# State-space stage of a hybrid transformer block: decay exponents from 16 contraction rows, both directions added before one mixing multiplication

## What is computed

```python
def ssd_chunked(x, dt, A, Bm, Cm):
    ...
    xdt = (x * dt[..., None]).reshape(b, c, CHUNK, G, r, P)
    adt = jnp.moveaxis((dt * A).reshape(b, c, CHUNK, G, r), 2, -1)
    a_cs = jnp.cumsum(adt, axis=-1)
    CB = jnp.einsum('bclgn,bcsgn->bcgls', Cc, Bc)
    Wd = CB[:, :, :, None] * segsum_exp(adt)
    y_diag = jnp.einsum('bcgrls,bcsgrp->bclgrp', Wd, xdt)
    ...
    return (y_diag + y_off).reshape(b, l, H, P)
...
    y_fwd = ssd_chunked(xs, dt[:, :, 0], A[0], Bm, Cm)
    y_bwd = fl(ssd_chunked(fl(xs), fl(dt[:, :, 1]), A[1], fl(Bm), fl(Cm)))
    y = y_fwd + y_bwd + d_skip.astype(f32)[:, None] * xs
```

## Time and profile before

| what | value |
|---|---|
| three runs | 2532.5, 2537.7, 2540.1 us (median 2537.7) |
| span of the profiled execution, first to last instruction | 2541.3 us |
| PE busy in it | 2338.2 us (92%) |
| DVE busy | 1483.2 us (58%) |
| ACT busy | 1006.7 us (40%) |
| POOL busy | 545.2 us (21%) |
| state-space stage | about 359 to 866 us of the span |

### The profile page before, as it was taken

How to read it: one execution, slowest core, us unless ns; L and a number is a source line. 1 busy time by engine, 2 the same in 40 slices (tenths; PEclk the granted TensorE clock), 3 DMA queues, 4 the chain that set the end, 5 groups by cost and what they waited for, 6 DMA issues and landing times.

```text
span 2541.3 us, 33250 instructions
## 1 busy us (share of the span) xinstructions
PE 2338.2 (92%) x12329; PEld 1957.3 (77%) x12329; DVE 1483.2 (58%) x2230; ACT 1006.7 (40%) x1608; POOL 545.2 (21%) x618
## 2 busy tenths in 40 slices
PE   7999989999999699989999999999988998969997
PEld 6887767888888587868888878997777887757774
DVE  3555456888888754354334434566736566456665
ACT  3354513444444432343223232555333335145553
POOL 1000004555556300000000000392234431012011
PEclk8999998999999899899999998999988999969999
DMA  5310221111211433122233230422010005249995
GB/s 185 100 59 9 68 83 50 50 50 56 71 54 50 158 108 100 50 83 72 95 100 100 83 128 23 133 84 75 26 50 1 1 1 184 83 184 371 417 412 204
DMA packets 166300, 267.49 MB, mean 105 GB/s; under 512 B 9033, under 2 KB 140441, under 8 KB 156313
## 3 DMA queue, kind: packets, MB, share of 16 engines
q1 hardware_dynamic: 161705, 249.45, 28.2%
q0 software_dynamic: 4464, 16.25, 1.7%
HBM read 237.38 MB, written 28.31 MB: 105 GB/s over the span
## 4 chain that ended last, share of the span: by engine, by line
PE 68%; DVE 13%; DVEq 6%; ACT 5%; issue 4%; POOL 1%; DMA 1%; POOLq 1%; ACTq 0%; SPq 0%
PE ps L176 16%; PE ps L178 16%; PE ps L177 16%; PE ps L3450 3%; DVE arena L1641 2%; PE ps L1003 1%; ACT pair L362 1%; PE ps L2860 1%; PE ps L2877 1%; PE ps L1025 1%; PE ps L606 1%; DVEq L1667 1%; DVE arena L1677 1%; DVEq L1640 1%; DVE ring_rounded L1628 1%
## 5 line engine op out<-in xcount | busy, mean ns | idle before, releaser
L178 PE MATMUL ps<-pair,pair 128*128 128x512 f32 (+1 forms) x2216 | 811.5, 366 | 0.0
L176 PE MATMUL ps<-pair,pair 128*128 128x512 f32 (+1 forms) x1960 | 737.4, 376 | 39.9 <-DVE pair L391 14.2
L177 PE MATMUL ps<-pair,pair 128*128 128x512 f32 (+1 forms) x1960 | 737.6, 376 | 0.0
L178 PEld LDWEIGHTS ps<-pair,pair 128*128 128x128 f32 x2216 | 427.7, 193 | 70.0
L176 PEld LDWEIGHTS ps<-pair,pair 128*128 128x128 f32 x1960 | 378.3, 193 | 103.7 <-issue 35.5
L177 PEld LDWEIGHTS ps<-pair,pair 128*128 128x128 f32 x1960 | 379.7, 194 | 69.5 <-issue 7.2
L362 ACT ACTIVATE pair<-ring 128x2048 fp32r<-128x2048 f32 x102 | 194.8, 1910 | 294.6 <-PE ps L178 288.0
L368 DVE TENSOR_TENSOR pair<-ring,pair 128x2048 fp32r<-128x2048 f32 x95 | 219.0, 2305 | 137.0 <-ACT pair L362 137.0
L1761 POOL TENSOR_TENSOR arena<-arena 128x256 f32<-128x256 f32 x128 | 91.4, 746 | 500.0 <-ACT arena L1538 500.0
L1753 POOL TENSOR_TENSOR pair<-arena,pair 128x512 fp32r<-128x512 f32 x128 | 156.2, 1249 | 58.4 <-PE ps L1409 58.3
L2127 POOL MEMSET arena<- 128x1 f32 x32 | 1.0, 98 | 660.7 <-DVEq L165 660.5
(11 more groups left out here) (525 smaller groups left out, 4003.6 us busy)
## 6 DMA issues: line engine op xcount, KB each, us to landing
ring<-in_w_in SPq DMA_DIRECT2D x54, 1024.0 KB, 6.5
arena<-in_w_exp_down SPq DMA_DIRECT2D x23, 1024.0 KB, 10.6
ring<-in_w_up SPq DMA_DIRECT2D x16, 1024.0 KB, 5.5
ring<-in_w_down SPq DMA_DIRECT2D x16, 1024.0 KB, 5.1
ring<-in_w_exp_gate SPq DMA_DIRECT2D x16, 1024.0 KB, 8.7
ring<-in_w_exp_up SPq DMA_DIRECT2D x16, 1024.0 KB, 10.7
expert_results<-arena SPq DMA_DIRECT2D x22, 512.0 KB, 11.0
ring<-in_w_in SPq DMA_DIRECT2D x16, 512.0 KB, 5.9
```

What stands on the lines that cost most here:

```text
L176: nc.tensor.matmul(out, lhs[1], rhs[0], start=start, stop=False)
L177: nc.tensor.matmul(out, lhs[0], rhs[1], start=False, stop=False)
L178: return nc.tensor.matmul(out, lhs[0], rhs[0], start=False, stop=stop)
```

## The change

The log decays are no longer spread over 512 columns by GpSimd. Their running sums inside a chunk are formed once, ahead of the stage (steps 4 and 5 beside the projection, now `Beside(6, ...)`), rounded in two parts, and stored by SyncE in 32 transfers as rows of a DRAM table whose frame of zeros and ones GpSimd makes in an earlier stage (`frame_pool`, stored by four transfers). For each chunk SyncE loads 16 rows of 1280 numbers. TensorE adds two products per direction: the identity times a triangle of large negative numbers, repeated for 4 heads, and the 16 rows against the 16 rows. The exponent also holds the logarithm of the step size, so the mixing needs the plain tokens `xt` and no step-weighted copy. GpSimd adds the two directions' exponentials (`both`) in place, VectorE multiplies the sum once by the unmasked C-B product (`mixer`), and TensorE mixes once per head.

`ex` has four slots instead of two, `M` two instead of four. The rest of the diff is the renaming of semaphores and the layout of the buffers.

```diff
+    def frame_pool(gp):
+        rates, ones_at = frame[:, 0:2 * GH * P], frame[:, 2 * GH * P:ROW]
+        gp.memset(rates, 0.0)
+        gp.memset(ones_at, 1.0)
+        gp.drain()
+        blocks = rates.rearrange("p (d r l) -> p d r l", d=2, r=GH)
+        for part in (2, 3):
+            gp.affine_select(out=blocks, in_=blocks, compare_op=ALU.not_equal, fill=1.0, base=-part * GH,
+                             pattern=[[0, 2], [-1, GH], [0, P]], channel_multiplier=1)
+            gp.drain()
+        gp.affine_select(out=ones_at, in_=ones_at, compare_op=ALU.is_ge, fill=0.0, base=2 * GH - 1,
+                         pattern=[[0, 2 * P]], channel_multiplier=-1)
+        gp.drain().then_inc(s_frame, 1)
...
     def store_gates(sp, k):
+        if k == 6:
+            sp.wait_ge(s_frame, 2)
+            for n in range(4):
+                whole = decay_rows.rearrange("(n k) x -> k n x", k=RANK)
+                sp.dma_start(whole[:, n * GROUPS:(n + 1) * GROUPS, :],
+                             frame.unsqueeze(1).to_broadcast([RANK, GROUPS, ROW])).then_inc(s_rows, 16)
...
+            dve.tensor_scalar(log_dt.rearrange("p c h -> p (c h)"), raw, 1e-30, None, ALU.max).then_inc(s_a_ready, 1)
...
+        if step == 5:
+            sums = ps[:, 7, :]
+            dve.wait_ge(s_a, 3)
+            dve.tensor_tensor(rounded[row_lo][forward, :], sums[forward, :],
+                              rounded[row_hi][forward, :].bitcast(F32), ALU.subtract)
...
+            act.activation(one_diag.hi[:, 0, :], core.ident, ACT.Copy)
+            act.activation(shut.hi[:, 0, :], GT, ACT.Copy, scale=NEG)
+            act.activation(shut.lo[:, 0, :], LT, ACT.Copy, scale=NEG)
+            act.wait_ge(s_a_ready, 2)
+            act.activation(log_dt.rearrange("p c h -> p (c h)"), log_dt.rearrange("p c h -> p (c h)"), ACT.Ln)\
+                .then_inc(s_a, 1)
...
+        if step == 5:
+            act.wait_ge(s_sums, 2)
+            act.activation(rounded[row_hi][forward, :], ps[forward, 7, :], ACT.Copy)
+            act.activation(rounded[row_hi][backward, :], ps[backward, 7, :], ACT.Copy, scale=-1.0).then_inc(s_a, 1)
+            act.activation(rounded[turn_lo][0:2 * H, :].bitcast(F32), ps[0:2 * H, 4, :], ACT.Copy).then_inc(s_a, 1)
+            act.wait_ge(s_a_ready, 3)
+            act.activation(rounded[turn_hi][0:2 * H, :], rounded[turn_lo][0:2 * H, :].bitcast(F32), ACT.Copy).then_inc(s_a, 1)
...
+        if step == 4:
+            pe.wait_ge(s_exp, 1)
+            pe.wait_ge(s_a, 2)
+            for d, (where, mask) in enumerate(((forward, LE), (backward, LT))):
+                for c in range(NT):
+                    nc.tensor.matmul(ps[where, 7, c * P:(c + 1) * P], a[:, d, c, :], mask, start=True, stop=True)
+            for c in range(NT):
+                mm = nc.tensor.transpose(ps[0:2 * H, 4, c * P:(c + 1) * P], log_dt[:, c, :], core.ident)
+            mm.then_inc(s_sums, 1)
...
-                     beside=Beside(4, pe=decay_tensor, act=decay_scalar, dve=decay_vector))
+                     beside=Beside(6, pe=decay_tensor, act=decay_scalar, dve=decay_vector))
...
+        def load_rows(g, c):
+            if c >= 2:
+                sp.wait_ge(diff_ready, g * 8 + (2 * c - 2))
+            else:
+                after(sp, diff_ready, g * 8 + (2 * c - 2))
+            src = decay_rows[columns((g * NT + c) * RANK, RANK), :]
+            sp.dma_start(row[0:RANK, c % 2, :].bitcast(F32), src).then_inc(row_landed[c % 2], 16)
+        def store_rows():
+            sp.wait_ge(s_a, 5)
+            sp.wait_ge(s_a_ready, 4)
+            sp.wait_ge(s_rows, 16 + 64)
...
+                    for n in range(2):
+                        at = c * chunk_of_rows + n * GH * ROW + d * GH * P
+                        sp.dma_start(bass.AP(decay_rows.tensor, at, [[group, GROUPS], [ROW + P, GH], [1, P]]),
+                                     rounded[(row_hi, row_lo)[n]][heads_at, t].bitcast(F32)).then_inc(s_rows, 16)
+                        at = c * chunk_of_rows + (2 + n) * GH * ROW + 2 * GH * P + d * P
+                        sp.dma_start(bass.AP(decay_rows.tensor, at, [[group, GROUPS], [ROW, GH], [1, P]]),
+                                     rounded[(turn_hi, turn_lo)[n]][heads_at, t].bitcast(F32)).then_inc(s_rows, 16)
...
+            sp.wait_ge(s_rows, 16 + 64 + 32 * 16)
...
+        store_rows()
+        core.begin(sp, before + 1)
+        load_rows(0, 0)
+        load_rows(0, 1)
...
+            load_rows(g, 2)
+            load_rows(g, 3)
+            load_rows(g + 1, 0)
+            load_rows(g + 1, 1)
...
-            pe.wait_ge(am_ready, g * 8 + (n + 1))
...
-            mask = (strict.hi, strict.lo)[n % 2][:, 0, :]
-            nc.tensor.matmul(ps[:, SUMS[n % 2], :], mask, am[n % 2].lo[:, 0, :], start=True, stop=False)
-            nc.tensor.matmul(ps[:, SUMS[n % 2], :], mask, am[n % 2].hi[:, 0, :], start=False, stop=True)\
-                .then_inc(diff_ready, 1)
+            nc.tensor.matmul(ps[:, SUMS[d], :].rearrange("p (r l) -> p r l", r=GH), one_diag.hi[:, 0, :],
+                             (shut.hi, shut.lo)[d].to_broadcast([P, GH, P]), start=True, stop=False)
+            if d == 0:
+                pe.wait_ge(row_landed[c % 2], g * 32 + (16 * (c // 2) + 16 + c % 2))
+            slot = row[0:RANK, c % 2, :]
+            nc.tensor.matmul(ps[:, SUMS[d], :], slot[:, 2 * GH * P + d * P:2 * GH * P + (d + 1) * P],
+                             slot[:, d * GH * P:(d + 1) * GH * P], start=False, stop=True).then_inc(diff_ready, 1)
...
-                    pe.wait_ge(xw_ready, g * 4 + 4)
...
                     nc.tensor.matmul(ps[:, 5, GW:2 * GW], fT[:, 3, t], prev[:, 1, c, :], start=True, stop=True)
-                pe.wait_ge(m_ready, g * 8 + (2 * c + 2))
+                pe.wait_ge(m_ready, g * 4 + (c + 1))
                 for r in range(GH):
-                    for d in range(2):
-                        mm = nc.tensor.matmul(ps[:, 7, r * 64:(r + 1) * 64],
-                                              M[:, (2 * c + d) % 4, r * P:(r + 1) * P],
-                                              xw[:, d, c, r * 64:(r + 1) * 64], start=d == 0, stop=d == 1)
+                    mm = nc.tensor.matmul(ps[:, 7, r * 64:(r + 1) * 64], M[:, c % 2, r * P:(r + 1) * P],
+                                          xt[:, c, r * 64:(r + 1) * 64], start=True, stop=True)
...
-            after(act, m_ready, g * 8 + (n - 1))
-            act.activation(ex[:, n % 2, :], ps[:, SUMS[n % 2], :], ACT.Exp).then_inc(ex_ready, 1)
+            if n >= 4:
+                act.wait_ge(m_ready, g * 4 + (n // 2 - 1))
+            act.activation(ex[:, n // 2 % 2, n % 2, :], ps[:, SUMS[n % 2], :], ACT.Exp).then_inc(ex_ready, 1)
...
-            for d, mask in enumerate((LE, GE)):
-                ins = dve.tensor_tensor(cb[:, d], ps[:, 3, :].rearrange("p (c n) -> p c n", c=NT),
-                                        mask.unsqueeze(1).to_broadcast([P, NT, P]), ALU.mult)
-            ins.then_inc(cb_read, 1)
+            dve.tensor_copy(cb, ps[:, 3, :].rearrange("p (c n) -> p c n", c=NT)).then_inc(cb_read, 1)
...
+        def mixer(g, c):
+            dve.wait_ge(xw_ready, g * 6 + (c + 3))
+            if c >= 2:
+                dve.wait_ge(y_ready, g * 4 + (c - 1))
+            dve.tensor_tensor(heads(M[:, c % 2, :]), heads(ex[:, c % 2, 0, :]),
+                              cb[:, c, :].unsqueeze(1).to_broadcast([P, GH, P]), ALU.mult)\
                 .then_inc(m_ready, 1)
...
-            mixers(g, 0)
-            mixers(g, 1)
+            mixer(g, 0)
             for c in range(NT):
                 if c + 1 < NT:
-                    mixers(g, 2 * c + 2)
-                    mixers(g, 2 * c + 3)
+                    mixer(g, c + 1)
...
+        def both(g, c):
+            gp.wait_ge(ex_ready, g * 8 + (2 * c + 2))
+            gp.tensor_tensor(ex[:, c % 2, 0, :], ex[:, c % 2, 0, :], ex[:, c % 2, 1, :], ALU.add)\
+                .then_inc(xw_ready, 1)
...
-            weighted(g, 2, wst)
-            weighted(g, 3, wst)
-            for n in range(2):
-                steps(g, n)
-            weighted(g, 0, dt)
-            weighted(g, 1, dt)
-            for n in range(2, 4):
-                steps(g, n)
+            weighted(g, 0, wst)
+            weighted(g, 1, wst)
+            both(g, 0)
+            both(g, 1)
...
             ins.then_inc(diag_done, 1)
-            for n in range(4, 8):
-                steps(g, n)
+            both(g, 2)
+            both(g, 3)
+        gp.wait_ge(s_rows, 16 + 64 + 32 * 16)
```

98 lines of the change are left out of this document (54 added, 44 removed).

## The result

| | before | after |
|---|---|---|
| eight runs each, median | 2533.4 us | 2547.9 us |
| lowest and highest | 2526.6, 2540.1 | 2542.6, 2549.8 |
| profiled execution's span | 2541.3 | 2546.1 |
| PE busy | 2338.2 us | 2335.4 us |
| DVE busy | 1483.2 us | 1397.7 us |

The ratio is 1.0054, with a 95% interval of [1.0040, 1.0068]: the changed kernel is some 14 us slower, where 3 us less was forecast. So the change costs 10 to 14 us, although VectorE is busy 86 us less and GpSimd 148 us less.

A forecast was written before the change was run, and what follows sets the result against it. VectorE was taken to set most of the round, with PE in it around chunks 0 and 1. Projection +8.5, loop -3.5 and last group -8.1 gave -3.1 us, from 2537.7 to 2535 (2530 to 2543); whole range 2510 to 2554.

The forecast's parts named there:

- the sums: PE's sums per chunk in the state-space stage: four products of 512 columns before and after, 0 us.
- the last group: Stage's last group, no features between chunks: from Y to the norm's end +27.3 instead of +35.4, -8.1 us.
- the round: One round of the stage's loop, from Y (start of PE's turn of y): 56.3 us at full clock, 4.0 less.
- Projection: Projection: PE stands still 9.6 us ahead of step 2, step 4 adds 2.4 us; +8.5, bounds 6 and 11.
- The table: DRAM table's frame, row stores and row loads: all hidden, 0 us, bound +3.
- Rival 4: Loop: GpSimd's additions hold up VectorE's convolutions, +1.3 us a round, +9 us, total 2544; chance 0.06.
- Clock: Loop: low PE clock behind gaps ahead of features 2 and the transposes costs 3.5 us a round, bounds 0 and 6.3.
- 27 us of low clock: Loop before the change: clock low after waits ahead of mixing in five of seven rounds, some 27 us in all.
- -0.5 a round: Loop: a round of 59.8 us, clock cost included; -3.5 us over seven rounds, bounds -28 and +16.

The follow-up runs named there:

- e1: Changed kernel with the 16 table rows padded with zeros to 128 for the decay-row products; 2535.1 us, ratio 0.9996.
- e2: Changed kernel with the projection's six side steps at pieces 1, 17, 33, 40, 46 and 54, the first three where they stood before; 2539.6 us, ratio 1.0012.
- e13: e6 with GpSimd making the table's frame only after the first gate is stored, and its stores issued one load later; 2493.3 us, ratio 0.9840.
- e11: Changed kernel with each chunk's two 128-row sums first and the two 16-row sums behind them; 2535.9 us, ratio 1.0007.
- e3: Changed kernel with GpSimd making the skip term before its addition for chunk 1, not behind it; 2517.0 us, ratio 0.9923.
- e6: Changed kernel with the edits of e1, e2 and e3 together; 2496.5 us, ratio 0.9861.
- e9: Changed kernel with eight products nobody reads on PE ahead of each feature product 2; 2532.9 us, ratio 0.9991.
- the second profile: Kernel before, unchanged, profiled once more; span 2526.3 us.
- the three edits: Padded rows, side steps where they stood and skip term first, together on the changed kernel; 2496.5 us, ratio 0.9861.
- e10: e6 with products nobody reads on PE in the last group, ahead of its waits for the states and each mixing; 2501.7 us, ratio 0.9857.

## Why the prediction was wrong, step by step

Three steps failed: the sums, put at 0 where they cost 8 us; the last group, walked at the full clock and 6.5 us too short; and the round, put 1.7 us too short at the full clock. Without the price of the 16 rows (e1) the changed kernel stands at 0.9996 [0.9981, 1.0011] of the kernel before, no slower than it; the forecast, with that term at 0, was 0.9988. That the two lie so close is partly luck: e1's last group is still 4 us longer than forecast, and its profile is 5 us or more shorter behind the stage.

- **Projection, +8.5 forecast: right, 7.3.** (Added up as written, its terms give 341.9 and 365.8, so +7.9.) PE stood still for 7.5 us instead of 9.6, and the new side work cost 1.9 for 2.4. The wait covers the 4 us that PE waited for a slab's weights before (e2); the walk has this only in its times, not as a term. What is left of the 5.4, some 1.9 us by difference, includes the low clock behind the wait (step 2 takes 2.93 us instead of 2.23).
- **The table, 0 with a bound of +3: 1.9 us.** The row stores were hidden, though they stood 0.70 us apart on SP's queue and not 0.43. At the start of the attention, where 1.3 of the 1.9 lie, it was the frame (e13): 0.9 us are GpSimd's selection beside VectorE's product. The other 0.6 stay open. I had looked at its DMAs and at who is idle, not at who works beside it.
- **Sums, 0 forecast: this step failed.** "Four products of 512 columns before and after" counts columns. Four took 1.60 us instead of 0.93, because two of them have 16 rows (e1, e11). It cost 5 us in the loop and 3 in the last group. With the skip term first it costs more: from e3 to e6 the mean round falls by 1.9 us, of which 0.8 in the rounds at the full clock (55.5 to 54.7).
- **Round at the full clock, 56.3 forecast: 58.0 (e9).** The walk was right in its order; its points came 0.6 to 1.3 us late and its end 1.7. Copy of feature product 0 at Y+10.9 instead of 10.2 (the first sums), y of chunk 0 at Y+17.7 instead of 17.1, part 2 at Y+25.4 instead of 24.1 (the 0.75 us that the addition took from convolution 0), PE's wait 2.6 instead of 3.3. Rival 4 had this mechanism and priced it at 1.3 us a round, but I gave it a chance of 0.06 as though it excluded the others.
- **Clock, 3.5 a round forecast: 2.3 (60.3 less 58.0).** The two errors of the round nearly cancel, by luck: 60.3 for 59.8. The prediction's 27 us of low clock before the change are those behind the mixing; in three of the six rounds it had also fallen by the 1.57 us wait ahead of the transposes.
- **The base.** The forecast of -0.5 a round was made against one profile, in which two early rounds took 61.2 us. In the second profile the mean was 59.5 instead of 60.0. Against the first profile alone the loop is 0.9 us longer; the other 2.6 of the 3.6 come from the second.
- **Last group, -8.1 forecast: -1.6. The largest miss.** I walked it at the full clock with handovers of 3.2 us a chunk. At half the clock PE needs 2.9 us for the sums of a chunk with their 16-row switches, 1.9 for the state products and 1.6 for mixing: 6.3 us a chunk, nearly without a wait. With 128 rows it is 31.3 us (e1), and mostly at the full clock, with the three edits, still 30.7 (e10). There y of the chunks starts at +11.6, +15.8, +20.4 and +24.5, where I had +11.4, +15.4, +18.6 and +21.1: in a group without features the chain of five steps takes over 4 us a chunk at the end, where I had 3.2 and 2.5.

Sum of the forecast: 8.5 - 3.5 - 8.1 = -3.1. Measured by stages: 7.3 + 1.9 + 3.6 - 1.6 = 11. The last group accounts for 6.5 of the 14 us between them, the loop for 7.1, the table for 1.9, and the projection takes 1.2 back.

The Trainium skill bears on both mechanisms. "SBUF — State Buffer", section "Who interferes with whom", makes a VectorE instruction with two SBUF inputs and a reading GpSimd instruction exclude each other; 1.50 for 0.75 us in convolution 0 and 1.45 for 0.55 at L1044 agree. "TensorE: Matmul & The Clock Gate", section "LDWEIGHTS (loading the stationary operand)", says that a load's time goes by the columns and not by the rows. The trace agrees (0.18 us for 16 rows, 0.19 for 128). The 0.14 to 0.17 us at each switch come on top of the load's own time.

What stays open: why the same wait of 2.6 us is followed by the low clock in one round and not in another, why e10 and e13 each had three rounds of 56.0 to 56.5 us, with the clock low by the transposes, where e6 had none, and what the other 0.6 us ahead of the projection are.

## What to carry to other kernels

Ask of every engine that is relieved what its work was in parallel with, and of each new helper what stands behind it on its queue: here one small product queued behind an addition decided some 30 us. A contraction of 16 rows between those of 128 was not free on TensorE; padding it with zeros took the price away, and grouping the thin ones more than half of it. And before a prediction of a few us is made against one profile, profile the same kernel twice.

## What the runs showed of the hardware

- A product over 16 rows between products over 128 of 512 columns costs 0.43 us from start to start instead of 0.23 at the full clock, and 0.72 instead of 0.43 at the low one. The weight load across such a switch isn't taken ahead of its product; between two 16-row products it is. Four sums take 1.60 us alternating, 1.21 grouped, 0.93 padded to 128 rows.
- Dead products in a 2.6 us wait kept the clock at 2.4 GHz in five of six rounds, also behind a second wait of 2.46 us that was left empty. In e6, waits of 1.2, 1.3 and 2.5 us a round did not lower it in five of six rounds.
- A VectorE step with its inputs in SBUF took 1.50 us instead of 0.75 beside a GpSimd addition, and 1.45 instead of 0.55 beside a GpSimd selection over 16 partitions.
- The small strided stores of the table left SP's queue 0.70 us apart, 32 of them in 23 us.
